# Window loads of the dilated sample stage requested inside the paged sample stage

## What is computed

```python
idx = n_buf + jnp.arange(t)[:, None] - dil * jnp.arange(n_keys + 1)[None, :]
kg, vg = k_all[:, idx], v_all[:, idx]
sc = jnp.einsum('bqhd,bqjhd->bhqj', q, kg).astype(jnp.float32) / math.sqrt(HEAD_DIM)
```

## Time and profile before

| what | us |
|---|---|
| median of three runs | 3229.28 |
| the profiled execution | 3229.47 |
| its span, first to last instruction | 3227.9 |
| paged stage, first gather to the request of the last store | 1929.2 to 2590.8 |
| window stage, first to last request on SP | 2593.7 to 2697.1 |
| merge, from | 2699.7 |

### The profile page before, as it was taken

The page is one execution under the profiler, slowest core; times in us unless marked ns, Lnnn a source line. Parts: engine busy times, 40 slices in busy tenths (PEclk is TensorE's granted clock), DMA queues, the critical chain, the costliest instruction groups (busy, mean ns, idle before and its releaser), DMA issues. The chain is left out here.

```text
span 3227.9 us, 47243 instructions
## 1 busy us (share of the span) xinstructions
PE 2910.8 (90%) x17678; PEld 2098.9 (65%) x17678; DVE 1674.2 (52%) x2736; ACT 1496.1 (46%) x2618; POOL 648.6 (20%) x959
## 2 busy tenths in 40 slices
PE   7999969999799999998999968888888773799998
PEld 5888848888555555554888855555555441588887
DVE  2000042322578888887666635555555434666663
ACT  4122142222477777776666624555555423333332
POOL 0000011212122222221033333344443200000000
PEclk9999989999899999999999979999999986899999
DMA  5444444445401010101233229999999886432321
GB/s 175 171 150 173 166 155 156 164 154 190 132 1 40 1 40 1 38 9 53 74 103 80 76 67 421 420 420 420 421 421 420 369 319 224 139 104 104 104 84 41
DMA packets 193925, 548.62 MB, mean 170 GB/s; under 512 B 30240, under 2 KB 99456, under 8 KB 157888
## 3 DMA queue, kind: packets, MB, share of 16 engines
q0 software_dynamic: 45568, 348.22, 27.5%
q1 hardware_dynamic: 148160, 197.75, 18.4%
HBM read 486.21 MB, written 126.68 MB: 190 GB/s over the span
## 5 line engine op out<-in xcount | busy, mean ns | idle before, releaser
L1464 DVE COPY sbs_kT<-sbs_ps_T 128x512 f32<-128x512 f32 x256 | 270.8, 1093 | 268.9 <-PE sbs_ps_T L1626 268.8
L418 PE MATMUL proj_ps_G<-proj_w_hi,proj_xT_hi 128*128 128x512 f32 x1024 | 402.4, 393 | 4.0 <-DVE proj_xT_lo L290 4.0
L422 PE MATMUL proj_ps_G<-proj_w_hi,proj_xT_lo 128*128 128x512 f32 x1024 | 399.5, 390 | 0.0
L420 PE MATMUL proj_ps_G<-proj_w_lo,proj_xT_hi 128*128 128x512 f32 x1024 | 399.4, 390 | 0.0
L362 ACT ACTIVATE proj_out<-proj_ps_G,proj_stat 128x512 f32<-128x512 f32 (+1 forms) x136 | 93.3, 688 | 567.3 <-PE proj_ps_G L422 562.6
L1626 PE MATMUL sbs_ps_T<-held,sbs_k_ring 128*128 128x128 f32 x2048 | 279.5, 292 | 43.0 <-ACT sbs_kT L1547 39.1
L290 DVE TENSOR_TENSOR proj_xT_lo<-proj_ps_T,proj_xT_hi 128x512 fp32r<-128x512 f32 (+1 forms) x68 | 42.2, 662 | 508.4 <-ACT proj_xT_hi L352 508.4
L1626 PEld LDWEIGHTS sbs_ps_T<-held,sbs_k_ring 128*128 128x128 f32 x2048 | 248.2, 153 | 86.3 <-ACT sbs_kT L1547 42.3
L626 POOL CAST sbp_sp_hi<-sbp_sp 128x512 fp32r<-128x512 f32 (+3 forms) x320 | 171.8, 551 | 505.8 <-DVE sbp_sp L668 499.8
L1547 ACT ACTIVATE sbs_kT<-sbs_ps_T 128x512 f32<-128x512 f32 x256 | 260.2, 1115 | 4.9 <-PE sbs_ps_T L1626 4.4
L668 DVE SCALAR_TENSOR_TENSOR sbp_sp<-sbp_Z,sbp_el 128x512 f32<-128x512 f32 (+3 forms) x320 | 179.9, 603 | 118.8 <-ACT sbp_el L746 118.5
(11 more groups left out here) (289 smaller groups left out, 5880.3 us busy)
## 6 DMA issues: line engine op xcount, KB each, us to landing
out_k_win_s<-in_cache_k_win POOLq DMA_DIRECT2D x16, 2044.0 KB, 8.5
out_v_win_s<-in_cache_v_win POOLq DMA_DIRECT2D x16, 2044.0 KB, 8.1
proj_out<-in_w_in SPq DMA_DIRECT2D x32, 512.0 KB, 5.3
proj_x_in<-in_x_prompt SPq DMA_DIRECT2D x32, 512.0 KB, 3.8
dls_k_in<-in_cache_k_win SPq DMA_DIRECT2D x16, 1024.0 KB, 10.2
dls_v_in<-in_cache_v_win SPq DMA_DIRECT2D x16, 1024.0 KB, 14.2
merge_o<-scratch_o_dil SPq DMA_DIRECT2D x48, 256.0 KB, 4.7
merge_x<-in_x_prompt SPq DMA_DIRECT2D x16, 512.0 KB, 4.5
```

Source lines behind the costliest of these rows:

```text
L418: nc.tensor.matmul(ps_G[0:n, g, :], xT_hi[:, slot, k, 0:n], w_hi[:, k, cols], start=(k == 0), stop=False)
L420: nc.tensor.matmul(ps_G[0:n, g, :], xT_hi[:, slot, k, 0:n], w_lo[:, k, cols], start=False, stop=False)
L422: mm = nc.tensor.matmul(ps_G[0:n, g, :], xT_lo[:, slot, k, 0:n], w_hi[:, k, cols], start=False, stop=(k == KC - 1))
L1464: nc.vector.tensor_copy(by_lane(kT[:, j, :, :])[:, :, i, :], ps_T[:, x % TB, :].rearrange("p (a n) -> p a n", a=PAIRS)).then_inc(kT_odd, 1)
```

## The change

The two rings are allocated outside of the stages and handed to both. In the paged stage SP requests, after its seventh store, the eight loads of keys of the window stage's first step, each into the ring slot that PE has just turned for the last time, then the first four loads of values once `av_done` is 31 and the other four once it is 32, and only then its eighth store. The window stage uses the rings in place of `k_in` and `v_in` (a slot for each set and entry), takes `ident` and `own` from the paged stage's constants, uses one `kT` for both sets, and requests only the second step's loads itself. The second clearing and barrier move behind the window stage.

```diff
-            for b in range(DEC_B):
+            def store(b):
                 sp.wait_ge(row_copied, b + 1)
                 sp.dma_start(t["o_sb_s"][b * DEC_S:(b + 1) * DEC_S, :], o_row[:, :]).then_inc(stored, 16)
+            for b in range(DEC_B - 1):
+                store(b)
+            for x in range(RING):
+                sp.wait_ge(k_turned, GP * (NC * N - RING + x + 1))
+                sp.dma_start(k_ring[:, x, :, :], window_chunk(t["cache_k_win"], x % NC, x // NC)).then_inc(win_k_loaded[x], 16)
+            for x in range(RING):
+                if x % NC == 0:
+                    sp.wait_ge(av_done, N - 1 + x // NC)
+                sp.dma_start(v_ring[:, x, :, :], window_chunk(t["cache_v_win"], x % NC, x // NC)) \
+                    .then_inc(win_v_loaded[x // NC], 16)
+            store(DEC_B - 1)
             sp.wait_ge(stored, 16 * DEC_B)
...
-        kT = m.sb("kT", [P, 2, E, PAIRS, 512])
+        kT = m.sb("kT", [P, E, PAIRS, 512])
...
                 if st > 0:
+                    for c in range(2):
+                        for e in range(E):
+                            sp.wait_ge(turned, tile_of(st - 1, c, e, NA - 1) + 1)
+                            sp.dma_start(k_ring[:, E * c + e, :, :], window_chunk(t["cache_k_win"], E * st + e, c)) \
+                                .then_inc(k_loaded[E * c + e], 16)
                     sp.wait_ge(av_done, st)
...
-                        if st > 0:
-                            eng.wait_ge(scored, 2 * (st - 1) + c + 1)
-                        copy(kT[:, c, e, :, n * P:(n + 1) * P], ps_T[:, tt % 3, :].rearrange("p (a n) -> p a n", a=PAIRS)) \
+                        if st + c > 0:
+                            eng.wait_ge(scored, 2 * st + c)
+                        copy(kT[:, e, :, n * P:(n + 1) * P], ps_T[:, tt % 3, :].rearrange("p (a n) -> p a n", a=PAIRS)) \
...
+            with nc.sbuf_tensor("sbs_k_ring", [P, 8, 4, W], F32) as k_ring, nc.sbuf_tensor("sbs_v_ring", [P, 8, 4, W], F32) as v_ring:
+                stick_breaking_sample(nc, t, held, paged_loaded, k_ring, v_ring, win_k_loaded, win_v_loaded)
+                dilated_sample(nc, t, held, k_ring, v_ring, win_k_loaded, win_v_loaded)
+        nc.clear_and_free_semaphores([dil_qk_loaded, paged_loaded] + win_k_loaded + win_v_loaded)
         nc.all_engine_barrier()
-        dilated_sample(nc, t)
```

More of the change, by code:

```diff
@@ L1280, in _, with window_chunk, stick_breaking_sample @@
                         turn_in(p + 1, f, OB[:, :])
-def stick_breaking_sample(nc, t, held, paged_loaded):
+def window_chunk(src, b, c):
+    rows = src[0].rearrange("b s h d -> b s (h d)")
+    if c == 0:
+        return rows[b, WIN - 512:WIN, :].rearrange("(n p) c -> p n c", p=P)
+    return rows[b].rearrange("(p r) c -> p r c", r=16)[:, 0:DEC_S, :]
+def stick_breaking_sample(nc, t, held, paged_loaded, k_ring, v_ring, win_k_loaded, win_v_loaded):
     C = H * DEC_S
@@ L1702, in _, with dilated_sample @@
             pick_rows(DEC_B - 1)
-def dilated_sample(nc, t):
+def dilated_sample(nc, t, held, k_ring, v_ring, k_loaded, v_loaded):
     C = H * DEC_S
@@ L1716, in dilated_sample @@
         m = Mem(nc, ctx, "dls")
-        ident = m.sb("ident", [P, P])
+        ident, own = (paged_constants(held)[n] for n in ("ident", "own"))
         mask = m.sb("mask", [P, KEYS])
         count = m.sb("count", [P, KEYS])
-        own = m.sb("own", [P, W])
         pick = m.sb("pick", [P, E * DEC_S])
-        qk_new = m.sb("qk_new", [NS, 2, W])
+        qk_new = held[0:NS, 2 * W:4 * W].rearrange("p (i c) -> p i c", c=W)
+        v_new = held[0:DEC_S, 4 * W:8 * W].rearrange("p (e c) -> p e c", c=W)
         q_pad = m.sb("q_pad", [P, DEC_B, PAIRS * (C + 8)])
@@ L1784, in _ @@
         def _(sp):
-            sp.dma_start(ident[:, :], t["ident"][:, :]).then_inc(new_loaded, 16)
             sp.dma_start(qk_new[:, 0, :], t["q_dl_s"]).then_inc(new_loaded, 16)
             sp.dma_start(qk_new[:, 1, :], k_new).then_inc(new_loaded, 16)
+            for buf, n in ((mask, "win_mask"), (count, "win_count"), (pick, "pick16")):
+                sp.dma_start(buf[:, :], t[n][:, :]).then_inc(consts, 16)
             for st in range(STEPS):
[L1789 to L1796, removed]
-                if st > 0:
-                    sp.wait_ge(av_done, st)
[L1799 to L1804, removed]
+                if st > 0:
+                    for c in range(2):
[3 more added lines that the diff above has]
+                                .then_inc(k_loaded[E * c + e], 16)
+                    sp.wait_ge(av_done, st)
+                    for c in range(2):
+                        for e in range(E):
+                            sp.dma_start(v_ring[:, E * c + e, :, :], window_chunk(t["cache_v_win"], E * st + e, c)) \
+                                .then_inc(v_loaded[c], 16)
+                sp.dma_start(v_new[:, :, :], v_new_d[E * st:E * st + E].rearrange("b s c -> s b c")) \
+                    .then_inc(v_new_loaded, 16)
                 if st > 0:
@@ L2474, in build @@
             dilated_prompt(nc, t, held, dil_qk_loaded, paged_loaded)
-            stick_breaking_sample(nc, t, held, paged_loaded)
-        nc.clear_and_free_semaphores([dil_qk_loaded, paged_loaded])
+            win_k_loaded = [nc.alloc_semaphore(name=f"win_k_loaded{x}") for x in range(8)]
+            win_v_loaded = [nc.alloc_semaphore(name=f"win_v_loaded{x}") for x in range(2)]
+            with nc.sbuf_tensor("sbs_k_ring", [P, 8, 4, W], F32) as k_ring, nc.sbuf_tensor("sbs_v_ring", [P, 8, 4, W], F32) as v_ring:
+                stick_breaking_sample(nc, t, held, paged_loaded, k_ring, v_ring, win_k_loaded, win_v_loaded)
+                dilated_sample(nc, t, held, k_ring, v_ring, win_k_loaded, win_v_loaded)
+        nc.clear_and_free_semaphores([dil_qk_loaded, paged_loaded] + win_k_loaded + win_v_loaded)
         nc.all_engine_barrier()
-        dilated_sample(nc, t)
         merge(nc, t)
```

24 lines of the change are left out of this document (6 added, 18 removed).

## The result

The changed kernel takes 3251.78 us (median of four runs, 3249.19 to 3253.17), against 3228.06 us before (four runs too; the three of the section on the time before are among them): the ratio is 1.0071, with a 95% interval from 1.0058 to 1.0085. That is 23 us slower, between 19 and 27. The profiled execution took 3249.19 us, its span is 3247.7 us. The forecast was 3248.5.

The account below looks back on a forecast made before the run. Paged stage bound by DMA, window stage by PE and softmax: + 21.8 (later window start) - 3.2 (its first step) + 0.6 (clearings ahead of merge) = + 19.2 us, so 3248.5 us; range 3240 to 3257.

Parts of the forecast that it names:

- The window stage is not bound by DMA, and early loads save little: Window stage: PE and the softmax chain set its time; early loads save 3.2 us in its first step.
- The DMA engines' total sets the paged stage's end: Paged stage's end: 32.1 MB at 420 GB/s keep the engines busy to 2612.5; the window stage starts 21.8 us later.
- The small store is held behind the loads: Paged stage's end: the 8 KB eighth store lands 2 us after the loads, at 2614.5, and everybody waits.
- Rival C: Paged stage's end: eighth store not held, lands in 1.6 us; 3226 to 3236 us; chance 0.07 slower, 0.10 within 6.5 us.
- The slip: Paged stage's last product: delayed by window loads served before gathered keys; below 14 us it leaves the end unchanged.
- the share between: Paged stage: DMA engines take queues in turn, so neither gathers nor window loads go first; slip some 10 us.
- The barriers: Between stages and ahead of merge: the second clearing moves behind the window stage, so 0.6 us only changes places.
- One `kT`: Window stage: set 1's copies wait for set 0's score, at no cost; 3.6 us a step if PE's order did not cover it.

Follow-up runs that it names:

- e11: The changed kernel run again unedited, as a second comparison with the kernel before: 3248.50 us, ratio 1.0063.
- e5: Changed kernel, but the eight key loads wait for turn 30's product and the values move to the window stage's start: 3229.82 us, ratio 0.9997.
- e2: Changed kernel with only the eight key loads left in the paged stage, values requested at the window stage's start: 3232.66 us, ratio 1.0013.
- e4: Changed kernel, but ACT issues the eighth store on its own DMA queue: 3250.68 us, ratio 1.0058.
- e7: Changed kernel, but the eighth store is issued ahead of the last four loads of values: 3246.36 us, ratio 1.0053.
- e6: Changed kernel with the window's last 512 rows read in larger packets, one output not as asked for, times only: 3250.49 us, ratio 1.0063.
- e9: Changed kernel without window loads in the paged stage, and with the first step's new values requested ahead of the masks: 3231.68 us, ratio 1.0006.
- e8: Changed kernel, but after turn 30's product only qk_new's two parts and four key loads are requested early: 3222.79 us, ratio 0.9977.
- e1: Changed kernel with no window load in the paged stage, only the restructuring left: 3233.99 us, ratio 1.0010.

## Why the prediction was right

The mechanism, the place and the size came out: the time lay 3.3 us above the forecast in the first comparison, and at it in the second. By the marks the parts are + 24.2 us to the window stage's first request, - 3.7 in it and + 0.4 to merge, together + 21.0; forecast were + 21.8, - 3.2 and + 0.6, together + 19.2. So the sum is not right by errors that cancel; its largest miss is the first part, 2.4 us.

- **The window stage is not bound by DMA, and early loads save little.** Forecast 103.4 to about 100 us, 3.2 us saved; it was 99.7 (97.9 in e11). The keys were turned 4.9 us after the first request, forecast 5.1, and the second set took 7.82 us, forecast 7.8. e5 saves 3.6, e2 3.5 us. Shown.
- **The DMA engines' total sets the paged stage's end.** Forecast: through at 2612.5, with no gap. The share is 1.01 to 1.04 up to 2606, 0.79 from 2606 to 2616. The store landed at 2616.8 (2601.20 + 0.33 + 15.3), forecast 2614.5, and the window stage started at 2617.97, forecast 2615.5. The term was sized 2.5 us too small: I took 420 GB/s to the end, where 394 and then 331 were moved. Two things lie in that. From 2596 to 2600 the full engines moved 1.53 MB in 751 packets (2.0 KB each), from 2606 to 2610 1.69 MB in 271 (6.2 KB each), so the same share carried fewer bytes in small packets; and in the last 6 us the engines ran out one after the other.
- **The small store is held behind the loads.** 15.3 us of wait instead of 1.1. e4 shows that it is the queue that holds it. The forecast left out what e4 and e7 showed: taking the store out of that place lets PE start only 3.3 or 2.8 us sooner, because the next stage's first inputs stand behind the same loads. Rival C priced an early landing at the slip less 3.2 us, here 7.8 - 3.2 = + 4.6 us; e4, which brings the early landing about, gave + 16.7. So the rival was priced 12 us too low.
- **The slip.** Between 0 and 14 us, with no effect on the end. It was 7.8 us, near the share between that the prediction put at some 10. e6 puts it to 20.5, and the window stage starts 4.4 us later (95.3 against 90.9), where 20.5 - 14 gives 6.5. e2 shows the other half, that without the values behind it the slip is paid in full.
- **The barriers.** Forecast 0.6 us later at merge; 0.4 (3.0 against 2.6).
- **One `kT`.** Forecast no cost. No row of the changed kernel or of e9 shows a wait for it.

The Trainium skill (DMA: Bandwidth & Descriptors, Queues, rings and completion order) has each DMA engine take its queues in turn, a packet at a time. The traces of the changed kernel and of e6, the first with two loaded queues, agree: 534 packets to 533 and 348 to 341 from 2540 to 2552, whatever their size, and bytes by the size. The same section's sentence that completion is not in order of issue was not seen at work here: the store landed with the end of the loads, after 15.6 us.

Left open: why the granted clock of the same products differs between executions of one kernel (the last product 9.75 us at 0.76 in the first execution of the changed kernel, 8.43 us at 0.85 in e11), and how the store's landing splits between the queue's order and the end of the loads' own last packets.

## What to carry to other kernels

Here a load that is requested early is free only in idle time of the DMA engines (e8), and in a stage whose time is DMA time it delays that stage's own loads (e2). At the end of a stage it also delays whatever small transfer the barrier waits for. Ask first what the next stage waits for with all its loads on time: here 7.6 us at its start, for 128 KB and one set of keys; request these alone, after the last gathers, and put small inputs ahead of large ones in each queue.

## What the runs showed of the hardware

- Two loaded queues shared the DMA engines by packets: from 2540 to 2552 packets of 2.0 KB beside those of 7.3 KB got a fifth of the bytes (1.06 of 4.97 MB), packets of 7.4 KB half of them (2.53 of 5.05 MB). The landing of the window's keys fell with it from 30.4 to 10.6 us in the median.
- SP itself is held while it requests: eight loads of 1024 KB, with no wait between them, took it 22.1 us in e1 with the engines full (share 1.03), and 7.0 us in the changed kernel's second step, where they idled before. In the changed kernel's first step it was 22.8 us, and SP reached its wait for the last product after that product's end. So a wait that follows them in program order is also reached late.
- For a load of 32 KB behind eight of 1024 KB PE waited 7.0 us in e1 (0.8 without it), and for a store of 8 KB behind eight the core waited 15.3 us, of which e4 and e7 win back about 3, because the next inputs stand in the same queue.
